# Last weight split of each residual product moved between the scalings of the layer norm, and the mean matmul of the down products four blocks later

## The chip, the cores and the metric

The kernel runs on one core of a Trainium2 chip. The metric is the device time of one execution in microseconds (us). The engines named below are TensorE (PE in the rows, with PEld for its weight loads), VectorE (DVE), ScalarE (ACT), GpSimd (POOL) and the queue of SyncE (SP), which issues the weight transfers.

## What is computed

Two transformer-like blocks run one after the other on 256 tokens of width 1024, all in float32. The first block has two layers, each with a mixer and a feed-forward part, and a layer norm behind each of the four:

```python
for i in range(DEPTH):
    mix = s5_mixer(h, ...) if i % N_MIXERS == 0 else stick_breaking_mixer(h, ...)
    h = layer_norm(DEEPNORM_ALPHA * h + mix, ln_mix_g[i], ln_mix_b[i])
    h = layer_norm(DEEPNORM_ALPHA * h + swiglu_ffn(h, ffn_w_gu[i], ffn_w_down[i]),
                   ln_ffn_g[i], ln_ffn_b[i])
```

The second block has two hybrid layers (window attention beside an mLSTM, then a squared-ReLU feed-forward) with RMS norms. The change touches the four layer norms of the first block alone. They are numbered n = 0 (behind the product with `ssm_w_out`), 1 (behind the first down product), 2 (behind `sb_w_o`) and 3 (behind the second down product).

## The kernel before

**Chunks.** Each weight matrix is cut into chunks of 128x2048 numbers, and one long series of chunks runs through the whole kernel. The raw ring has three slots (`RING = 3`). SyncE loads a chunk into `raw` (`load_chunk`, L362). ScalarE rounds it to `w_hi` (`split_hi`, L395) once the product that used the slot is done. VectorE computes `w_lo = raw - w_hi` (`split_lo`, L400). TensorE needs both: each product is made of three matmuls, high by high, high by low and low by high (L419 to L421), or of two where the moving operand holds both parts (L429, L430). A load waits until the `w_lo` of the chunk that had the slot before is made. So chunk c's product releases the split of chunk c + 3.

**The residual products.** `ssm_out` and `sb_out` have 4 chunks, `down0` and `down1` 11. Each chunk is worked off in 16 blocks of 128 columns (`resid_blocks`). Eight tiles `res` (128x256) come out. `resid_lo(dve, g, idx)` makes the `w_lo` of chunk idx + 3, counted from the product's first: for the last chunk this is the third chunk of the product that follows the layer norm. VectorE's order is written out by hand in `resid_vector` (L1241).

**The layer norm.** It begins before its product ends. With four tiles done VectorE adds them (`shift_sum`, L1048 and L1050). TensorE turns this sum into a provisional mean (`shift_mean`, L786, one float32 matmul over `prod`), and VectorE subtracts that from all tiles (`shifted_tiles`, L1056 and L1058) before the last four tiles arrive. Once the eighth tile is there, TensorE sums differences and squares (`layer_norm_tensor`, L808 to L818), and ScalarE takes them up: L886 squares the mean difference into `rstd`, L887 copies it to `dm_sb`. VectorE forms the variance (L1124), ScalarE the reciprocal root (L891, L894). Then `layer_norm_vector` runs over four pairs of tiles, each op 128x512:

- `centre(q)`, L1129: `xn` minus `dm_sb`; VectorE waits for its own result behind it
- `scale(q)`, L1134: `xn` times `rstd`. ScalarE's `normed_pair` then writes `res` (L919) and, for the first two pairs, `x_hi` (L928)
- `high(q)`, L1142 and `low(q)`, L1150: `x_hi` of the last two pairs, and `x_lo` of all. For n = 3 these are two ops a pair (L1140, L1119)
- `split(0)`, `split(1)`: the `w_lo` of the chunks four and five of the next product. Their `w_hi` comes from `early_columns` (L936 to L940), which stands behind all four `normed_pair` on ScalarE
- `normalised(0)`, `normalised(1)`, L1162 and L1168: what is left of the two early products

**TensorE meanwhile.** While the norm is computed it multiplies the two first chunks of the next product by tiles that are not yet normalised (`early_tensor`, on `raw_hi` and `raw_lo`). Then comes the third chunk, block by block as `x_lo` arrives; its `w_lo` is the one of the split that the change moves. After it comes the fourth, which needs `split(0)`. Behind the fourth chunk n = 1 has the first scores of the attention (L1324), which need `normalised` of both early products; n = 3 has the gate products (L2363), some chunks later.

Of the kernel before, what the change touches and what calls it, by code (L numbers as in the profile page):

```python
# [246 lines left out]
def stack(nc, w, out):  # L247
# [4 lines left out]
    with ctx:  # L252
# [144 lines left out]
        def split_lo(dve, c, idx, k):  # L397
            s = (c + k) % RING
            dve.wait_ge(hi_done, idx + (c + 1))
            nc.vector.tensor_tensor(w_lo[s][:, :], raw[s][:, :], w_hi[s][:, :].bitcast(F32), ALU.subtract).then_inc(lo_done, 1)  # L400
# [291 lines left out]
        def resid_lo(dve, g, idx):  # L692
            if g.c0 + idx + RING < n_chunks:
                split_lo(dve, g.c0 + RING, idx, idx % RING)
# [88 lines left out]
        def shift_mean(pe, n):  # L783

            pe.wait_ge(s_done, n + 1)
            nc.tensor.matmul(PS[:, 3, 0:T], C("mean_c"), prod[:, 0:T], start=True, stop=True).then_inc(shift_ready, 1)  # L786
# [37 lines left out]
        def resid_tensor(pe, g, n, first=True):  # L824

            if g.shape == "kt8":
                if g.half:
                    for kts in ((0, 4), (4, 6), (6, KT)):
                        for idx in range(2):
                            resid_first(pe, g, kts, idx)  # L830
                elif first:
                    resid_first(pe, g)
                if not g.half:
                    resid_blocks(pe, g, 1)
                if n < 4:
                    resid_blocks(pe, g, 2, 0, 6)
                    shift_mean(pe, n)
                    resid_blocks(pe, g, 2, 6, 16)
                else:
                    resid_blocks(pe, g, 2)  # L840
                resid_blocks(pe, g, 3)
            else:
                for idx in range(g.n):
                    if n < 4 and idx == 6:
                        shift_mean(pe, n)
                    resid_blocks(pe, g, idx)
            if n < 4:
                first = 4 if n in (0, 2) else 5
                early_tensor(pe, n, 0, (0, first))
                layer_norm_tensor(pe, n)  # L850
                early_tensor(pe, n, 0, (first, KT))
                early_tensor(pe, n, 1)
# [269 lines left out]
        def layer_norm_vector(dve, g, n):  # L1122
            dve.wait_ge(rstd_done, 3 * n + 2)
            nc.vector.tensor_tensor(rstd[:, :], PS[:, 3, T:2 * T], rstd[:, :], ALU.subtract).then_inc(v_done, 1)  # L1124
            twice = [t[:, :].unsqueeze(1).to_broadcast([P, 2, T]) for t in (dm_sb, rstd)]

            def centre(q):
                pair = xn[:, 2 * q:2 * q + 2, :]
                nc.vector.tensor_tensor(pair, pair, twice[0], ALU.subtract).then_inc(dve_step, 1)  # L1129
                dve.wait_ge(dve_step, v_count.one())  # L1130

            def scale(q):
                pair = xn[:, 2 * q:2 * q + 2, :]
                nc.vector.tensor_tensor(pair, pair, twice[1], ALU.mult).then_inc(scaled, 1)  # L1134

            def high(q):
                dve.wait_ge(res_normed, KT * n + 2 * q + 2)
                if n == 3:
                    for t in (2 * q, 2 * q + 1):
                        nc.vector.tensor_scalar(x_hi[:, t, :], res[:, t, :], gain(4, t), None, ALU.mult).then_inc(xh_done, 1)  # L1140
                    return
                nc.vector.tensor_copy(x_hi[:, 2 * q:2 * q + 2, :], res[:, 2 * q:2 * q + 2, :]).then_inc(xh_done, 2)  # L1142

            def low(q):
                if n == 3:
                    gained_lo(dve, 4, 2 * q)
                    gained_lo(dve, 4, 2 * q + 1)
                    return
                dve.wait_ge(xh_done, KT * x_index(n) + 2 * q + 2)
                nc.vector.tensor_tensor(x_lo[:, 2 * q:2 * q + 2, :], res[:, 2 * q:2 * q + 2, :],  # L1150
                                        x_hi[:, 2 * q:2 * q + 2, :].bitcast(F32), ALU.subtract).then_inc(xl_done, 2)

            def split(slot):
                e, idx = early_chunks(n)[slot]
                split_lo(dve, e.c0 + RING, idx, idx)

            def normalised(slot):

                e, idx = early_chunks(n)[slot]
                dve.wait_ge(cols_copied, 2 * n + slot + 1)  # L1160
                for m in range(2):
                    ins = nc.vector.scalar_tensor_tensor(out=early[:, slot, m * T:(m + 1) * T], in0=dm_sb[:, :],  # L1162
                                                         scalar=col_sums[:, 2 * slot + m, 0:1],
                                                         in1=early_banks(slot)[:, m, 0:T], op0=ALU.mult, op1=ALU.add)
                ins.then_inc(dve_step, 1)
                dve.wait_ge(dve_step, v_count.one())
                both = early[:, slot, :].rearrange("p (a t) -> p a t", a=2)
                nc.vector.tensor_tensor(both, both, twice[1], ALU.mult).then_inc(early_done, 1)  # L1168

            centre(0)  # L1170
            dve.wait_ge(rstd_done, 3 * n + 3)
            scale(0)
            for q in range(1, 3):
                centre(q)
                scale(q)
            low(0)
            centre(3)
            scale(3)
            low(1)
            high(2)  # L1180
            low(2)
            high(3)
            low(3)
            split(0)
            split(1)
            if n == 3:
                square_sums(dve, 4, 0, 4)
            normalised(0)
            normalised(1)
            if n in (0, 2):  # L1190
                early_gated(dve, n, 0)
                early_gated(dve, n, 1)
# [48 lines left out]
        def resid_vector(dve, g, n):  # L1241
            last = g.n - 1
            held = 2 if g.shape == "kt8" else last
            if g.half:
                half_vector(dve, g, n)
                return
            raw_columns(dve, n)
            if n == 3:
                gate_weights(dve)
            for idx in range(g.n):  # L1250
                for t in range(KT):
                    if g.ends[t][0] != idx:
                        continue
                    if n < 4 and t == 4:
                        shifted_tiles(dve, g, n)
                    if n < 4 and t >= 4:
                        shifted_tile(dve, g, n, t)
                    else:
                        add_tile(dve, g, t)
                    if n < 4 and t == 3:  # L1260
                        dve.wait_ge(resid_done, g.resid0 + 4)
                        shift_sum(dve, n)
                        raw_columns_lo(dve, g, n)
                    if n < 4 and t == 5:
                        pair_shift(dve, n)
                    if n in (1, 3) and t == 7:
                        fold_mean(dve, n, 7)
                    if n < 4 and t >= 4:
                        raw_tile_lo(dve, n, 2 * t - 8)
                        raw_tile_lo(dve, n, 2 * t - 7)  # L1270
                    if n == 6:
                        gained_lo(dve, n, t)
                        if t == 5:
                            square_sums(dve, n, 0, 2)
                        if t == 7:
                            square_sums(dve, n, 2, 4)
                    if n < 4 and t == 5:
                        add_squares(dve, n, 0)
                    if n < 4 and t == 6:
                        square_sums(dve, n, 1, 3)  # L1280
                        fold_mean(dve, n, 6)
                    if n in (0, 2) and t == 7:
                        fold_square(dve, n, 6)
                    if n in (1, 3) and t == 7:
                        fold_square(dve, n, 6)
                        fold_square(dve, n, 7)
                if n >= 4 or idx < held:
                    resid_lo(dve, g, idx)
            if n < 4:
                for idx in range(held, g.n):  # L1290
                    resid_lo(dve, g, idx)
            if n < 4:
                layer_norm_vector(dve, g, n)


# [1846 lines left out]
```

## Time and profile before

| | |
|---|---|
| median of 3 runs | 1345.09 us (1344.32 to 1345.76) |
| the profiled execution | 1345.14 us |
| its span in the profile | 1343.3 us |
| TensorE matmuls busy | 1314.0 us (98%) |
| VectorE busy | 944.0 us (70%) |
| ScalarE busy | 676.2 us (50%) |
| GpSimd busy | 56.7 us (4%) |
| share of the chain that ended last: TensorE, VectorE, ScalarE | 86%, 7%, 4% |
| data moved | 227.81 MB, 170 GB/s |

Times in the rows are us from the start of the span. TensorE is busy nearly throughout, so the question for any edit is where TensorE waits, and what ends last before it goes on. A row of the timeline with "x2" holds two instructions back to back. The time given is that of both, and an instruction may start a little before the one ahead of it has ended. The text calls the time from one start to the next a step.

### The profile page before, as it was taken

To read this page: it belongs to the slowest core of one execution; us is meant where nothing else is said; L and a number is where in the kernel's file an instruction comes from. 1 tells how busy PE (TensorE), PEld (TensorE's weight loads), DVE (VectorE), ACT (ScalarE), POOL (GpSimd) and SP (SyncE) were. 2 spreads that over 40 slices of the span, in tenths; PEclk is the share of its full clock that TensorE was granted. 3 is DMA by queue.
4 is the path that set the end of the run, shared out by engine and by line. 5 is a ranking of instruction groups with operands and counts; after the bars stand their busy time and mean duration, and the time that the engine had idled before them with its cause. 6 is when DMAs were issued, how large, how long until landed. Compare 5 with 4: busy or idle time off the path is not lost.

```text
span 1343.3 us, 25869 instructions
## 1 busy us (share of the span) xinstructions
PE 1314.0 (98%) x10699; PEld 1245.2 (93%) x10699; DVE 944.0 (70%) x1340; ACT 676.2 (50%) x838; POOL 56.7 (4%) x31
## 2 busy tenths in 40 slices
PE   5899999999999999999999999999999999999999
PEld 4599999988999999998989999998898999999988
DVE  8966976657865986657897788775457867877542
ACT  5774643334765653344666545444445554544332
POOL 6910000000000000000000000000000000000000
PEclk9999999999999999999999999999999999999999
DMA  8676486675443576666444456567664535556662
GB/s 157 158 185 185 133 221 184 188 190 180 145 148 96 157 208 185 187 188 176 153 137 147 155 159 217 189 184 192 188 188 127 157 123 192 189 188 187 188 188 63
DMA packets 342809, 227.81 MB, mean 170 GB/s; under 512 B 22616, under 2 KB 337792, under 8 KB 342592
## 3 DMA queue, kind: packets, MB, share of 16 engines
q1 hardware_dynamic: 341200, 226.33, 58.5%
q8 instruction: 67, 1.10, 0.3%
q10 hardware_dynamic: 1520, 0.20, 0.1%
q14 instruction: 22, 0.18, 0.0%
HBM read 224.40 MB, written 1.05 MB: 168 GB/s over the span
## 4 chain that ended last, share of the span: by engine, by line
PE 86%; DVE 7%; ACT 4%; issue 1%; POOL 1%; SPq 0%; DMA 0%; DVEq 0%; ACTq 0%; POOLq 0%
PE PS L419 20%; PE PS L420 20%; PE PS L421 20%; PE PS L429 12%; PE PS L430 6%; DVE w_lo L400 2%; ACT w_hi L395 1%; PE PS L1340 1%; DVE xn L1134 1%; DVE xn L1129 1%; DMA c_rows<-in_ssm_c_re_dram 0%; PE PS L1742 0%; PE PS L2430 0%; PE PS L1324 0%; DVE raw_lo L1089 0%
## 5 line engine op out<-in xcount | busy, mean ns | idle before, releaser
L400 DVE TENSOR_TENSOR w_lo<-raw,w_hi 128x2048 fp32r<-128x2048 f32 x207 | 473.6, 2291 | 144.1 <-ACT w_hi L395 143.3
L419 PE MATMUL PS<-x_hi,w_hi 128*128 128x256 f32 x1792 | 504.1, 281 | 1.0 <-DVE w_lo L400 0.5
L420 PE MATMUL PS<-x_lo,w_hi 128*128 128x256 f32 x1792 | 503.7, 281 | 0.0
L421 PE MATMUL PS<-x_hi,w_lo 128*128 128x256 f32 x1792 | 503.3, 281 | 0.0
L395 ACT ACTIVATE w_hi<-raw 128x2048 fp32r<-128x2048 f32 x207 | 396.4, 1915 | 203.2 <-PE PS L430 139.1
L419 PEld LDWEIGHTS PS<-x_hi,w_hi 128*128 128x128 f32 x1792 | 338.3, 189 | 6.0 <-issue 2.9
L420 PEld LDWEIGHTS PS<-x_lo,w_hi 128*128 128x128 f32 x1792 | 336.6, 188 | 0.1
L421 PEld LDWEIGHTS PS<-x_hi,w_lo 128*128 128x128 f32 x1792 | 336.6, 188 | 0.0
L429 PE MATMUL PS<-hid_both,w_hi 128*128 128x512 f32 x756 | 264.8, 394 | 0.0
L430 PE MATMUL PS<-hid_both,w_lo 128*128 128x256 f32 x756 | 211.8, 280 | 0.0
L429 PEld LDWEIGHTS PS<-hid_both,w_hi 128*128 128x128 f32 x756 | 142.1, 188 | 31.4
L430 PEld LDWEIGHTS PS<-hid_both,w_lo 128*128 128x128 f32 x756 | 142.4, 188 | 0.1
L420 PE MATMUL PS<-hid_both,w_hi 128*128 128x256 f32 x492 | 138.3, 281 | 0.0
L421 PE MATMUL PS<-hid_both,w_lo 128*128 128x256 f32 x492 | 138.2, 281 | 0.0
L419 PE MATMUL PS<-hid_both,w_hi 128*128 128x256 f32 x492 | 137.8, 280 | 0.0
L419 PEld LDWEIGHTS PS<-hid_both,w_hi 128*128 128x128 f32 x492 | 92.9, 189 | 0.9 <-issue 0.7
L420 PEld LDWEIGHTS PS<-hid_both,w_hi 128*128 128x128 f32 x492 | 92.4, 188 | 0.1
L421 PEld LDWEIGHTS PS<-hid_both,w_lo 128*128 128x128 f32 x492 | 92.4, 188 | 0.0
L616 ACT ACTIVATE gate_sb<-PS 128x256 f32<-128x256 f32 x48 | 18.4, 383 | 139.5 <-PE PS L421 138.2
L619 ACT ACTIVATE gate_sb<-gate_sb 128x512 f32<-128x512 f32 x32 | 20.2, 632 | 96.0 <-DVE gate_sb L672 96.0
L659 DVE TENSOR_TENSOR prod<-PS,gate_sb 128x256 f32<-128x256 f32 x48 | 20.3, 424 | 58.6 <-ACT gate_sb L616 58.6
L704 DVE SCALAR_TENSOR_TENSOR res<-res,PS 128x256 f32<-128x256 f32 x48 | 19.7, 419 | 35.5 <-PE PS L430 20.0
(395 smaller groups left out, 1482.1 us busy)
## 6 DMA issues: line engine op xcount, KB each, us to landing
raw<-in_w_ff_dram SPq DMA_DIRECT2D x128, 512.0 KB, 4.5
raw<-in_ffn_w_gu_dram SPq DMA_DIRECT2D x88, 512.0 KB, 5.1
raw<-in_w_in_dram SPq DMA_DIRECT2D x68, 512.0 KB, 4.6
raw<-in_sb_w_qkv_dram SPq DMA_DIRECT2D x24, 512.0 KB, 4.5
raw<-in_ffn_w_down_dram SPq DMA_DIRECT2D x20, 512.0 KB, 4.5
raw<-in_ssm_w_glu_dram SPq DMA_DIRECT2D x16, 512.0 KB, 5.6
raw<-in_w_out_dram SPq DMA_DIRECT2D x16, 512.0 KB, 4.6
raw<-in_ssm_w_out_dram SPq DMA_DIRECT2D x8, 512.0 KB, 4.5
```

Source lines behind the costliest of these rows:

```text
L395: nc.scalar.activation(w_hi[s][:, :], raw[s][:, :], ACT.Copy).then_inc(hi_done, 1)
L400: nc.vector.tensor_tensor(w_lo[s][:, :], raw[s][:, :], w_hi[s][:, :].bitcast(F32), ALU.subtract).then_inc(lo_done, 1)
L419: nc.tensor.matmul(dst, lhs_hi, r_hi, start=start, stop=False, skip_group_check=True)
L420: nc.tensor.matmul(dst, lhs_hi, r_lo, start=False, stop=False, skip_group_check=True)
L421: return nc.tensor.matmul(dst, lhs_lo, r_hi, start=False, stop=stop, skip_group_check=True)
L429: nc.tensor.matmul(PS[:, bank, :], lhs_hi, both.rearrange("p i t -> p (i t)"), start=start, stop=False, skip_group_check=True)
L430: return nc.tensor.matmul(PS[:, bank, 0:T], lhs_lo, both[:, 0, :], start=False, stop=stop, skip_group_check=True)
L616: nc.scalar.activation(gate_sb[:, k, 0:T], PS[:, bank, T:2 * T], g.func).then_inc(sig_done, 1)
L619: nc.scalar.activation(gate_sb[:, k, :], gate_sb[:, k, :], ACT.Square).then_inc(u_done, 1)
L659: nc.vector.tensor_tensor(prod[:, 0:T], PS[:, bank, 0:T], gate_sb[:, k, 0:T], ALU.mult).then_inc(z_done, 1)
L704: ins = nc.vector.scalar_tensor_tensor(out=res[:, t, :], in0=res[:, t, :], scalar=g.alpha, in1=PS[:, tile_bank(g, t), 0:T], op0=ALU.mult, ...
L1129: nc.vector.tensor_tensor(pair, pair, twice[0], ALU.subtract).then_inc(dve_step, 1)
```

## The change

For all four layer norms, the `w_lo` of the last chunk of the residual product (`resid_lo` of index g.n - 1) is no longer made before `layer_norm_vector`, but inside it, behind the scalings of pairs 0 and 1. The order inside becomes centre 0, centre 1, scale 0, scale 1, the split, centre 2, scale 2, low 0, low 1, centre 3, scale 3, high 2 and so on. For the down products (n = 1 and 3), `shift_mean` moves from ahead of chunk 6 to behind its first four blocks.

```diff
@@ resid_tensor
                 for idx in range(g.n):
                     if n < 4 and idx == 6:
+                        resid_blocks(pe, g, idx, 0, 4)
                         shift_mean(pe, n)
-                    resid_blocks(pe, g, idx)
+                        resid_blocks(pe, g, idx, 4, 16)
+                    else:
+                        resid_blocks(pe, g, idx)
@@ layer_norm_vector
             centre(0)
+            centre(1)
             dve.wait_ge(rstd_done, 3 * n + 3)
             scale(0)
-            for q in range(1, 3):
-                centre(q)
-                scale(q)
+            scale(1)
+            resid_lo(dve, g, g.n - 1)
+            centre(2)
+            scale(2)
             low(0)
+            low(1)
             centre(3)
             scale(3)
-            low(1)
             high(2)
             low(2)
             high(3)
@@ resid_vector
             if n < 4:
-                for idx in range(held, g.n):
+                for idx in range(held, last):
                     resid_lo(dve, g, idx)
-            if n < 4:
                 layer_norm_vector(dve, g, n)
```

## Rows read from the trace of the kernel before

**Rows 1.** The page, busy time of each engine and its share of the span.
```profile
PE 1314.0 (98%) x10699; PEld 1245.2 (93%) x10699; DVE 944.0 (70%) x1340; ACT 676.2 (50%) x838; POOL 56.7 (4%) x31
```

**Rows 2.** Waits of TensorE: line, whom it waited for, total us, times, longest.
```profile
PE PS L786 <- DVE prod L1050: 1.5, 2, 0.7
...
PE PS L2363 <- ACT rstd L894: 0.4, 1, 0.4
```

**Rows 3.** Timeline of TensorE, n = 1: start, duration, line, op, [idle before].
```profile
303.83 0.28 PE L430 MATMUL PS<-hid_both,w_lo 128*128 128x256 f32 x1
...
304.18 0.28 PE L430 MATMUL PS<-hid_both,w_lo 128*128 128x256 f32 x1
305.19 0.70 PE L786 MATMUL PS<-prod,const 128*128 128x256 f32 x2 [0.73 <-DVE prod L1050]
```

**Rows 4.** Timeline of TensorE, the same mean matmul for n = 0.
```profile
133.46 0.28 PE L421 MATMUL PS<-hid_both,w_lo 128*128 128x256 f32 x1
133.58 0.59 PE L786 MATMUL PS<-prod,const 128*128 128x256 f32 x2
```

**Rows 5.** Timeline of VectorE, n = 1, behind the provisional mean.
```profile
308.66 1.28 DVE L1056 TENSOR_TENSOR xn<-res,PS 128x512 f32<-128x512 f32 x2
```

**Rows 6.** Timeline of VectorE, n = 0, through the layer norm.
```profile
146.39 4.49 DVE L400 TENSOR_TENSOR w_lo<-raw,w_hi 128x2048 fp32r<-128x2048 f32 x2
150.80 0.42 DVE L1124 TENSOR_TENSOR rstd<-PS,rstd 128x256 f32<-128x256 f32 x1
...
152.32 0.69 DVE L1134 TENSOR_TENSOR xn<-xn,rstd 128x512 f32<-128x512 f32 x1 [0.50 <-ACT rstd L894]
152.93 0.69 DVE L1129 TENSOR_TENSOR xn<-xn,dm_sb 128x512 f32<-128x512 f32 x1
153.65 0.69 DVE L1134 TENSOR_TENSOR xn<-xn,rstd 128x512 f32<-128x512 f32 x1
...
156.91 0.69 DVE L1134 TENSOR_TENSOR xn<-xn,rstd 128x512 f32<-128x512 f32 x1
```

**Rows 7.** Timeline of ScalarE, n = 0.
```profile
148.31 0.38 ACT L887 ACTIVATE dm_sb<-PS 128x256 f32<-128x256 f32 x1
151.26 0.51 ACT L891 ACTIVATE rstd<-rstd,const 128x256 f32<-128x256 f32 x1 [2.57 <-DVE rstd L1124]
...
158.74 1.92 ACT L395 ACTIVATE w_hi<-raw 128x2048 fp32r<-128x2048 f32 x1
```

**Rows 8.** Timeline of TensorE, n = 0, first matmul of the fourth chunk.
```profile
163.03 0.39 PE L419 MATMUL PS<-x_hi,w_hi 128*128 128x256 f32 x1 [0.26 <-DVE w_lo L400]
```

**Rows 9.** Timeline of VectorE, n = 1, through the layer norm.
```profile
339.21 0.42 DVE L1124 TENSOR_TENSOR rstd<-PS,rstd 128x256 f32<-128x256 f32 x1
...
345.31 0.69 DVE L1134 TENSOR_TENSOR xn<-xn,rstd 128x512 f32<-128x512 f32 x1
...
349.09 4.49 DVE L400 TENSOR_TENSOR w_lo<-raw,w_hi 128x2048 fp32r<-128x2048 f32 x2 [0.22 <-ACT w_hi L395]
```

**Rows 10.** Timeline of ScalarE, n = 1.
```profile
338.58 0.38 ACT L887 ACTIVATE dm_sb<-PS 128x256 f32<-128x256 f32 x1
...
356.64 0.91 ACT L953 ACTIVATE qkv<-early,col_sums 128x256 f32<-128x256 f32 x2 [0.60 <-DVE early L1168]
```

**Rows 11.** Timeline of TensorE, n = 1, first scores.
```profile
357.60 0.70 PE L1324 MATMUL PS<-qkv 64*128 64x256 f32 x4
```

**Rows 12.** Timeline of VectorE, n = 3, the last scale and the next splits.
```profile
654.67 0.69 DVE L1134 TENSOR_TENSOR xn<-xn,rstd 128x512 f32<-128x512 f32 x1
...
658.70 4.49 DVE L400 TENSOR_TENSOR w_lo<-raw,w_hi 128x2048 fp32r<-128x2048 f32 x2
```

**Rows 13.** Timeline of TensorE, n = 3, first matmul of the fourth chunk.
```profile
661.04 0.39 PE L419 MATMUL PS<-x_hi,w_hi 128*128 128x256 f32 x1
```

**Rows 14.** The page, DMA issues: name, queue, count, KB each, us to landing.
```profile
raw<-in_ffn_w_gu_dram SPq DMA_DIRECT2D x88, 512.0 KB, 5.1
```

**Rows 15.** Busy time by stretch: us, busy of each engine, TensorE's clock, DMA share, GB/s.
```profile
54.00:66.00 12.00, 8.61 (x120) 5.91 (x119) 11.72 (x68) 11.31 (x15) 10.31 (x4) 1.00 0.58 138
```

## The prediction

> **What bounds the kernel now.** I read the busy shares first. TensorE is busy 98% of the span, VectorE 70%, ScalarE 50% [rows 1], so VectorE's work costs only where TensorE has run out of work in front of it. Then come TensorE's waits. Around the layer norms few are left: 1.5 us in two pieces before the provisional mean of the down products, on VectorE's sum, and 0.4 us before the gate products of n = 3, on a reciprocal root that closes VectorE's chain [rows 2]. The timelines around each norm give the rest. In n = 0, TensorE gets to the fourth chunk and waits for its low half: the matmul starts at 163.03 with idle time before it [rows 8], and n = 2 repeats this. In n = 3 the fourth chunk starts at 661.04 [rows 13], 0.05 behind the end of its `w_lo` (658.70 + 2.29, half of the pair's 4.49 and a little [rows 12]). In n = 1 the first scores at 357.60 start 0.05 behind the end of ScalarE's last early eviction (356.64 + 0.91) [rows 10, 11]. So in all four norms the chain that TensorE ends up waiting for is one and the same: VectorE's centrings and scalings, ScalarE's `normed_pair` 3, ScalarE's next `w_hi`, VectorE's next `w_lo`. What moves the last scaling, `scale(3)`, moves TensorE.
>
> **Part 1, the mean matmul.** Now TensorE starts the last matmul ahead of it at 304.18 and the mean at 305.19, a step of 1.01 with 0.73 marked idle [rows 3]. Unstalled, in n = 0, that step is 133.58 - 133.46 = 0.12 [rows 4]. The wait is 1.01 - 0.12 = 0.89. One block takes 304.18 - 303.83 = 0.35 [rows 3], so four blocks are 1.40 of work put into a wait of 0.89. It goes wholly, with 0.5 to spare, and the two other steps around the float32 matmul stay, once. What is late next: the mean comes out 1.40 - 0.89 = 0.5 later. VectorE takes it up at 308.66 at the earliest [rows 5], because the split of chunk 5 is queued before; the mean is done at about 305.19 + 0.70, and 0.5 more leaves over 2 us. So nobody is late. Gain 0.89 in n = 1 and the same in n = 3, whose wait is the other half of the 1.5 [rows 2]: **-1.8**.
>
> **Part 2, the split.** A split holds VectorE for a step of (150.80 - 146.39) / 2 = 2.20 [rows 6]. It leaves the place before L1124 and comes back between `scale(1)` and `centre(2)`. I follow the start of `scale(3)`.
>
> n = 0 (n = 2 is the same). (a) L1124 starts at 150.80, as soon as the second split is through. Its input from ScalarE ends at 148.31 + 0.38 = 148.69 [rows 7], and 0.1 passes until VectorE can start. It could start at 148.79, since the first split ends at about 148.6 [rows 6]: -2.01. (b) VectorE idles 0.50 before `scale(0)`; an op that waits for its own predecessor leaves 153.65 - 152.93 - 0.69 = 0.03 anyway, so `centre(1)` fills 0.47 [rows 6]. It covers the root: that is ready 152.32 - 150.80 = 1.52 behind L1124's start, and `scale(0)` now comes 0.33 + 2 x 0.72 = 1.77 behind it (0.72 = 153.65 - 152.93; 0.33 = 152.32 - 0.47 - 0.72 - 150.80) [rows 6]. -0.47. (c) The split: +2.20. (d) `low(1)` goes ahead of `centre(3)`; an op of 128x512 behind which nothing waits has a step of 152.93 - 152.32 = 0.61 [rows 6]: +0.61. Sum: -2.01 - 0.47 + 2.20 + 0.61 = **+0.33**. `scale(3)` goes from 156.91 to 157.24; `w_hi` starts 158.74 - 156.91 = 1.83 behind it [rows 6, 7], as nothing else holds ScalarE, and TensorE's 163.03 becomes 163.36. What goes on the way are short waits for `x_lo` inside the third chunk. They don't count, as TensorE only waits longer at the fourth. Two norms: **+0.7**.
>
> n = 1. The step that pays in n = 0 is missing. L1124 starts at 339.21 [rows 9] behind one split, but its input ends at 338.58 + 0.38 = 338.96 [rows 10] and can be used at 339.06. The split lies beside ScalarE's and TensorE's work now; without it VectorE stands idle there. (a) is -0.15, (b) -0.47, (c) +2.20, (d) +0.61: **+2.19**. `scale(3)` goes from 345.31 to 347.50, the splits from 349.09 to 351.28 [rows 9], the last eviction and the scores by as much, 357.60 to 359.79 [rows 10, 11]. TensorE gets to the fourth chunk about when its `w_lo` is there now (349.09 + 2.29 = 351.38), so it already loses this time there.
>
> n = 3. The same, but `low` is two smaller ops. (d) I take as 0.8, between the 0.61 of one op and twice the 0.42 of L1124's size [rows 6]. `scale(3)` then goes 2.4 later. The next `w_lo` starts 658.70 - 654.67 = 4.03 behind it now [rows 12]; in n = 0 and 1 ScalarE's `w_hi` allows 1.83 + 1.92 + 0.03 = 3.78 [rows 6, 7, 9], so 0.25 is VectorE's own queue and is given back: **+2.15**, less nothing, since TensorE stands at this `w_lo` already [rows 13]. The gate products' root follows from the same chain, so their wait neither grows nor absorbs.
>
> Other users of the moved split. Its own product, the third chunk, starts in n = 0 no earlier than its `x_lo`, and the split is done about 2 us before; in n = 1 it ends at 344.3 and the chunk starts at about 345.8. Its end also frees a slot for a load on SyncE's queue: 3.2 later in n = 0, 5.1 in n = 1. The load lands in 5.1 [rows 14], and ScalarE reads it only in the third split behind the norm, behind those that start at 158.74 [rows 7]. The loads queued after it each wait for a later split anyway. I take 0, at most 0.5 a norm.
>
> **The sum.** 0.33 + 2.19 + 0.33 + 2.15 - 1.78 = +3.2. The profiled execution took 1345.14 for a span of 1343.3, which becomes 1346.5, so 1348.4. The median of the runs, 1345.09, is 0.05 below: 1348.3. The terms that no row shows are VectorE's pick-up time (0.03 to 0.15 for each norm) and the step of `low` for n = 3 (0.61 to 0.84): together 1347.8 to 1348.9.
>
> **The rivals.** *A, the cover holds in part.* In n = 1 and 3 the third chunk's waits for `x_lo` and the later chain overlap more kindly than I add, or in n = 0 and 2 the split costs nothing because the fourth chunk's idle (0.26 marked [rows 8]) goes: 0.3 each there, 0.25 each in n = 1 and 3. For it: in n = 0 the sum is a difference of larger numbers. Against: every step is from a row. 3.2 - 1.1 = +2.1: 1347.2. *B, faster.* In n = 1 and 3 TensorE has work in front for the whole 2.2, and the wait stays hidden. Then part 1 alone is left: 1345.1 - 1.8 + 0.7 = 1344.0, and 1343.3 if n = 0 and 2 are free too. It decides from a cover of 1.3 us a norm. For it: TensorE has two early chunks and the third in front. Against: it starts the fourth in n = 3 right at the end of `w_lo` [rows 12, 13], and in n = 1 no wait could be that short by chance at the scores [rows 10, 11]. The cover is 0. *C, part 1 gives nothing:* the sum is later too, or TensorE runs into the next wait: 1350.1. Against: VectorE's tile 3 hangs on a block that lies before. *D, the clock.* In the stretch in which TensorE is busy 8.61 of 12.00 us its granted clock stays 1.00, the higher level of 2.4 GHz [rows 15]; the new waits are 2.2 us in pieces. If it fell, the third chunk (48 matmuls, about 5.7) at half speed would add 5.7 in n = 1 and 3: 1360. The Trainium skill, "TensorE: Matmul & The Clock Gate", Part 1 on the clock gate, says that the clock drops to its lower level once TensorE has been idle; by that rule longer waits would be paid twice. The stretch above doesn't show a drop after idle time of this size, and the sum is made without it.
>
> **How the numbers follow.** Forecast 66% (1347.8 to 1348.9, 1348.3), A 20%, B 5%, C 8%, D 1%. About 0.2%, 2.7 us, is what a measurement of this kernel can tell from no change, so slower begins at 1347.8. Slower: 66% less 3 at the edge, plus C and D, 72%. Same: A and the edge, 23%. Faster: B, 5%. The range leaves out B, D and the top of C: 1346.6 to 1349.6.
>
> **What would show it.** TensorE's wait at L786 gone in n = 1 and 3, with the mean's first user unmoved. L1124 2.0 earlier in n = 0 and 2 behind L887, 0.15 earlier in n = 1 and 3, with VectorE idle for over 2 us before it. The wait at the fourth chunk 0.3 longer in n = 0 and 2. In n = 1 and 3 a new wait of about 2 us before the fourth chunk, on `w_lo`. Wrong would be: the fourth chunk of n = 1 starting less than 1 us later against L887 than now, a split under 2 us, or a clock below 1.00.

## The result and the profile after

The changed kernel takes 1348.0 us (median of 14 runs, 1346.84 to 1349.81), the kernel before beside it 1345.34 us (14 runs, 1344.32 to 1345.94). The ratio is 1.0019, with a 95% interval of 1.0012 to 1.0026: slower by 2.7 us, where +3.2 was forecast. Its own profiled execution took 1346.84 us for a span of 1345.0.

The page has the same busy times to within 1.4 us, against [rows 1]. The work is the same, and what changed is who waits:

```profile
span 1345.0 us, 25869 instructions
PE 1314.3 (98%) x10699; PEld 1246.6 (93%) x10699; DVE 944.5 (70%) x1340; ACT 676.7 (50%) x838; POOL 56.8 (4%) x31
```

TensorE's waits (line, whom it waited for, total us, times, longest). The wait of L786 [rows 2] is gone. In its place stand four waits for `w_lo`, one before the fourth chunk of each norm:

```profile
PE PS L419 <- DVE w_lo L400: 4.5, 4, 1.3
...
PE PS L2367 <- ACT rstd L897: 0.4, 1, 0.4
```

The kernel before had two such waits, in n = 0 and 2:

```profile
PE PS L419 <- DVE w_lo L400: 0.5, 2, 0.3
```

Lines behind L840 are three or four higher than before: L1127 is the old L1124, L1132 and L1137 are `centre` and `scale`, L1153 is `low`.

TensorE at the mean matmul of n = 1. The step to L786 is 0.12 now, where it was 1.01 [rows 3], and the one behind it 0.24:

```profile
304.64 0.28 PE L430 MATMUL PS<-hid_both,w_lo 128*128 128x256 f32 x1
304.76 0.59 PE L786 MATMUL PS<-prod,const 128*128 128x256 f32 x2
305.00 0.58 PE L429 MATMUL PS<-hid_both,w_hi 128*128 128x512 f32 x1
```

VectorE in n = 0, which answers to [rows 6]. The second split no longer stands before L1127. It comes behind the two scalings, and VectorE waits for nobody up to `centre(3)`:

```profile
145.18 2.29 DVE L400 TENSOR_TENSOR w_lo<-raw,w_hi 128x2048 fp32r<-128x2048 f32 x1
147.51 0.43 DVE L1127 TENSOR_TENSOR rstd<-PS,rstd 128x256 f32<-128x256 f32 x1
147.85 1.41 DVE L1132 TENSOR_TENSOR xn<-xn,dm_sb 128x512 f32<-128x512 f32 x2
149.29 1.29 DVE L1137 TENSOR_TENSOR xn<-xn,rstd 128x512 f32<-128x512 f32 x2
150.50 2.29 DVE L400 TENSOR_TENSOR w_lo<-raw,w_hi 128x2048 fp32r<-128x2048 f32 x1
...
154.03 1.29 DVE L1153 TENSOR_TENSOR x_lo<-res,x_hi 128x512 fp32r<-128x512 f32 x2
155.24 0.69 DVE L1132 TENSOR_TENSOR xn<-xn,dm_sb 128x512 f32<-128x512 f32 x1
155.96 0.69 DVE L1137 TENSOR_TENSOR xn<-xn,rstd 128x512 f32<-128x512 f32 x1
```

VectorE in n = 1, against [rows 9]. The place that the split left is now idle time, 2.78 us:

```profile
337.14 0.42 DVE L1127 TENSOR_TENSOR rstd<-PS,rstd 128x256 f32<-128x256 f32 x1 [2.78 <-ACT dm_sb L890]
...
340.14 2.29 DVE L400 TENSOR_TENSOR w_lo<-raw,w_hi 128x2048 fp32r<-128x2048 f32 x1
...
345.60 0.69 DVE L1137 TENSOR_TENSOR xn<-xn,rstd 128x512 f32<-128x512 f32 x1
```

TensorE at the fourth chunk of n = 0, 1 and 3. The marked idle time was 0.26 in n = 0 [rows 8] and none in n = 3 [rows 13]. In n = 1 it was none either, as the row behind these three, from the kernel before, shows:

```profile
162.08 0.38 PE L419 MATMUL PS<-x_hi,w_hi 128*128 128x256 f32 x1 [1.02 <-DVE w_lo L400]
...
351.72 0.39 PE L419 MATMUL PS<-x_hi,w_hi 128*128 128x256 f32 x1 [1.15 <-DVE w_lo L400]
...
662.74 0.39 PE L419 MATMUL PS<-x_hi,w_hi 128*128 128x256 f32 x1 [1.35 <-DVE w_lo L400]
```

```profile
351.66 0.28 PE L419 MATMUL PS<-x_hi,w_hi 128*128 128x256 f32 x1
```

**Where the time went, stage by stage.** Both kernels issue the same 10699 matmuls. So one can take the start of the same matmul in two traces and subtract. The difference at seven places (100, 170, 330, 370, 480, 640 and 690 us of the kernel before) gives what each stage, the stretch between two of them, added. A minus sign is time gained. "n=0" to "n=3" are the stages with the four layer norms, "mean1" and "mean3" those with the mean matmul of the two down products. The first number is the lead or lag with which the first block's products are reached, before anything that was changed. Worked out in this way, in us against the trace of before:

```
kernel        at 100    n=0   mean1    n=1    n=2   mean3    n=3   behind 690
changed        -1.21  +0.25  -0.95  +2.19  +0.27  -0.99  +2.15   +0.00
after_again    -0.24  +0.25  -0.96  +2.21  +0.26  -0.98  +2.15   +0.05
mean_only      +1.18  -0.01  -0.94   0.00   0.00  -0.95  +0.01    0.00
split_only     -0.11  +0.27  +0.15  +2.21  +0.26  +0.14  +2.15   +0.02
keep13         -0.52  +0.25  -0.95  +1.36  +0.27  -0.99  +1.07   +0.03
low_back       -0.12  -0.35  -0.97  +1.59  -0.31  -1.00  +1.59   -0.03
joined         +0.26  -0.35  -0.97  +0.07  -0.34  -0.98  +0.09    0.00
centre_mean    +0.75  +0.07  -0.97  +0.06  +0.06  -0.95  +0.08   +0.03
keep02         +1.17  +1.36  -0.99  +2.20  +1.36  -0.99  +2.13   +0.01
best           -0.37  -0.33  -0.97  +0.01  -0.34  -0.98  +0.02    0.00
```

For the changed kernel the stages add up to 0.25 - 0.95 + 2.19 + 0.27 - 0.99 + 2.15 = +2.92. Less the lead of 1.21 at the start, that is the +1.7 between the two spans. The medians differ by 2.7.

### The profile page after: what moved, and what is told of

Same layout as the page of the kernel before. It is cut to its first block, busy times and chain, and to the rows that moved or that the text cites. A ratio compares the mean times of both kernels' runs of the same rounds, so it can differ in the third digit from the quotient of the medians.

```text
span 1345.0 us, 25869 instructions
## 1 busy us (share of the span) xinstructions
PE 1314.3 (98%) x10699; PEld 1246.6 (93%) x10699; DVE 944.5 (70%) x1340; ACT 676.7 (50%) x838; POOL 56.8 (4%) x31
## 3 DMA queue, kind: packets, MB, share of 16 engines
HBM read 224.40 MB, written 1.05 MB: 168 GB/s over the span
## 4 chain that ended last, share of the span: by engine, by line
PE 89%; DVE 7%; ACT 3%; issue 1%; DMA 0%; SPq 0%; DVEq 0%; ACTq 0%
PE PS L419 21%; PE PS L420 21%; PE PS L421 21%; PE PS L429 13%; PE PS L430 7%; DVE w_lo L400 1%; ACT res L922 1%; PE PS L1344 1%; DVE xn L1132 1%; DVE run L2267 1%; ACT w_hi L395 1%; DVE xn L1137 1%; DVE PS L2215 0%; DVE terms L2262 0%; DVE lag L2200 0%
```

## The experiments

Each was timed beside the kernel before, of which the medians were 1345.26 for the first four, 1345.31 for the next four and 1345.51 for the last. Ratios are to the kernel before, with their 95% interval.

**The mean matmul alone.** The kernel before with the first hunk of the diff.

> Only the mean matmul of the down products moves, the split stays where it was. Theory (the four norms carry the slowdown, the mean matmul gives back): the wait of 0.89 us before L786 goes in n = 1 and 3, and nothing is late for it: 1.8 to 1.9 us faster than the kernel before, and TensorE 0.9 to 1.0 ahead from n = 1 on. Rival C (the wait only moves on): within 0.3 us of before, with a new wait on TensorE or VectorE behind the mean.

Measured: 1343.39, ratio 0.9985 (0.9976 to 0.9994), so 1.9 us faster. Both mean stages give 0.94 to 0.95, and no other stage moves by more than 0.01. Rival C falls.

**The split alone.** The changed kernel without the first hunk.

> Only the split and the two reorderings in the layer norm, the mean matmul stays. Theory: +0.3 in n = 0 and 2, +2.2 in n = 1 and 3, so 4.8 to 5.0 us slower than before. Rival A (cover in part): 3.7 to 4.0. Rival B (hidden in n = 1 and 3): under 1.

Measured: 1350.36, ratio 1.0034 (1.0022 to 1.0046), 5.1 us slower. The four norms are those of the changed kernel. A and B fall. The stages of the two mean matmuls lose 0.15 each, in many small steps and not at L786; the cause is open.

**The split kept in its old place in n = 1 and 3.**

```diff
@@ resid_vector
-                for idx in range(held, last):
+                for idx in range(held, last if n in (0, 2) else g.n):
                     resid_lo(dve, g, idx)
@@ layer_norm_vector
             scale(1)
-            resid_lo(dve, g, g.n - 1)
+            if n in (0, 2):
+                resid_lo(dve, g, g.n - 1)
```

> The changed kernel, but in n = 1 and 3 the split stands again before L1127, where VectorE idles for 2.8 us; n = 0 and 2 and the mean matmul stay as changed. Theory (the idle time there is what made the old place free): each of n = 1 and 3 gives back about 2.05 of its 2.2; against before +0.27 twice, +0.1 twice and -1.9, so 1.1 to 1.3 us faster than before and about 4 faster than the change. Rival (the cost lies in the reordering of centrings and low(1), not in the split): no more than 1.5 us faster than the change, so still slower than before.

Measured: 1346.53, ratio 1.0009 (1.0000 to 1.0018). That is 1.3 slower than before, at the edge of no change, where 1.2 faster was expected. Against the changed kernel it is 1.65 faster, so the rival's number (1.5 at most, still slower than before) is the nearer one. Its reading is borne out too: the run joined, below, only puts `low(1)` back and takes away nearly all of what is left in n = 1 and 3. n = 1 and 3 still cost 1.36 and 1.07 where 0.1 was expected. VectorE's timeline in n = 1 shows why:

```profile
341.70 0.69 DVE L1137 TENSOR_TENSOR xn<-xn,rstd 128x512 f32<-128x512 f32 x1
342.41 0.69 DVE L1153 TENSOR_TENSOR x_lo<-res,x_hi 128x512 fp32r<-128x512 f32 x1
344.12 0.69 DVE L1153 TENSOR_TENSOR x_lo<-res,x_hi 128x512 fp32r<-128x512 f32 x1 [1.02 <-ACT x_hi L931]
344.73 0.69 DVE L1132 TENSOR_TENSOR xn<-xn,dm_sb 128x512 f32<-128x512 f32 x1
```

`low(1)` ahead of `centre(3)` costs its own 0.61 only as long as `x_hi` of pair 1 is there. With the split in front it was. Without it VectorE stands 1.02 us at `low(1)`, and `centre(3)` behind it stands too. So half of what leaving out the split would give is taken by another wait: a new one, in a place where the changed kernel has none.

**The changed kernel once more.**

> The changed kernel once more, beside the others on the same chip. Its profiled execution was 1.2 us ahead before the first norm was reached. Theory (chance in the first 70 us): another execution differs there by up to a microsecond either way, and every norm shows the same steps as before: about +0.3, +2.2, +0.3, +2.15 and twice -0.95. Rival (the change speeds up the start): the start is ahead again by 1.2 us. Time 2.5 to 3.2 us over before.

Measured: 1348.18, ratio 1.0020 (1.0011 to 1.0029), 2.9 us slower. Every stage up to 690 us repeats to within 0.02, and at 100 us the lead is 0.24 and not 1.21. So the start differs by chance, and the change doesn't speed it up. A part of what differs is in TensorE's clock. Here is the first profiled execution of the changed kernel (stretch, busy of each engine, TensorE's clock, DMA share, GB/s), behind a wait of 2.98 us for a transfer:

```profile
61.94 2.95 PE L1818 MATMUL PS<-toep,u_in 128*32 128x128 f32 x49 [2.98 <-DMA toep<-toep]
```

```profile
62.00:64.00 2.00, 2.00 (x40) 2.00 (x44) 1.97 (x14) 1.95 (x3) 1.92 (x2) 0.50 0.37 65
64.00:66.00 2.00, 2.00 (x65) 2.00 (x61) 1.89 (x3) 1.91 (x4) 0.64 (x1) 0.78 0.00 0
344.00:354.00 10.00, 8.59 (x70) 8.11 (x69) 9.03 (x11) 5.82 (x10) 0.00 (x0) 1.00 0.41 133
655.00:665.00 10.00, 8.37 (x67) 7.97 (x68) 9.51 (x16) 8.19 (x15) 0.00 (x0) 1.00 0.37 116
```

The clock stood at 0.50 there, the lower level of 1.2 GHz, and at 1.00 in the norms of n = 1 and 3. In after_again and in the kernel before it stayed at 1.00 between 54 and 76 us. Of the eleven traces of this study it fell between 60 and 73 us in six.

What a fall costs can be read in single traces. In mean_only the 96 matmuls of L1835 take 4.49 us from 68.70 on, with the clock at 0.50 from 70 to 72 us, where the kernel before takes 2.87 for the same work (its L1832) at 1.00. Measured by the same matmul in both traces, mean_only is 0.10 behind ahead of them and 1.18 behind at 100 us. Measured in the same way, the fall costs 1.05 in centre_mean, 0.34 in joined, 0.20 in keep02 and 0.10 in split_only. keep02 had another fall at about 30 us and was 1.4 behind at 40 us. The lead of the changed kernel doesn't come from the clock: it was 1.15 ahead at 59 us, before its clock fell. So the clock is a part of the spread and not the whole of it.

**low(1) behind scale(3) again.**

```diff
             low(0)
-            low(1)
             centre(3)
             scale(3)
+            low(1)
```

> The changed kernel with low(1) behind scale(3) again; split and mean matmul as changed. Theory (everything ahead of scale(3) on VectorE moves the fourth chunk one for one): scale(3) comes 0.61 earlier in n = 0, 1 and 2 and 0.80 in n = 3, where VectorE's own queue keeps 0.35 of it back: 0.6 three times and 0.45, so 2.2 to 2.3 us faster than the change, 0.3 to 0.8 slower than before. Rival (TensorE is held by x_lo, so a later low(1) costs what it gives): within 0.5 of the change.

Measured: 1345.73, ratio 1.0003 (0.9994 to 1.0013), 0.4 slower than before and 2.3 faster than the change. By stage 0.60, 0.60, 0.58 and 0.56 come back. The theory holds for the first three to within 0.03; n = 3 gave 0.56 for 0.45. So `x_lo` of pair 1 does not set the end of these stages. The time itself can't be told from that of the kernel before.

**Both: the split moved in n = 0 and 2 alone, and low(1) back.**

> As keep13 (the split moved in n = 0 and 2 alone), but with low(1) behind scale(3) again. In keep13 VectorE idled 1.02 and 0.92 us before low(1), until ScalarE had written x_hi of pair 1. Theory (low(1) ahead of centre(3) costs 0.6 where the split fills that time, and 1.7 where it doesn't): scale(3) comes 1.7 earlier than in keep13 in n = 1 and 3 and 0.6 in n = 0 and 2; against before -0.3 twice, -0.3, -0.5 and -1.9 for the mean matmul, so 3.0 to 3.5 us faster than before. Rival (the early stage of n = 1 and 3 is bound elsewhere): no more than 2.5 faster than before.

Measured: 1342.46, ratio 0.9979 (0.9970 to 0.9988), 2.85 faster than before: a little less than expected. n = 0 and 2 give 0.35, as expected, but n = 1 and 3 give nothing (+0.07, +0.09) where 0.3 and 0.5 were expected from `centre(1)`. The stages add up to -2.5, which is the rival's figure: n = 1 and 3 are held by something else, and the next run shows by what.

**centre(1) ahead, nothing else inside the norm.** The kernel before with the mean matmul moved and:

```diff
             centre(0)
+            centre(1)
             dve.wait_ge(rstd_done, 3 * n + 3)
             scale(0)
-            for q in range(1, 3):
-                centre(q)
-                scale(q)
+            scale(1)
+            centre(2)
+            scale(2)
```

> The kernel before with the mean matmul moved and centre(1) ahead of the wait for the root; the split stays where it was in all four norms, low(1) too. Theory (step a and c of the prediction cancel to +0.2 in n = 0 and 2, so the split's new place is worth nothing anywhere, and only centre(1) gives something): -0.47 in n = 0, 2 and 3, -0.3 in n = 1, where the early eviction waits no more and TensorE's own work sets the scores, -1.9 for the mean: 3.4 to 3.8 us faster than before. Rival (the split's place gives something in n = 0 and 2): slower than the run joined by 0.5 or more.

Measured: 1343.67, ratio 0.9989 (0.9979 to 0.9998), 1.6 faster than before, and the mean matmul's 1.9 is all of that. The expectation was out by 1.8 at least: `centre(1)` ahead costs 0.06 to 0.08 in each norm. The rival holds, as this kernel is 1.2 slower than joined. VectorE in n = 0 did get ahead. From L1127 to `scale(3)` it takes 5.76 here (151.55 to 157.31), against 6.11 before (150.80 to 156.91 [rows 6]). But ScalarE's `w_hi` doesn't follow:

```profile
151.55 0.42 DVE L1127 TENSOR_TENSOR rstd<-PS,rstd 128x256 f32<-128x256 f32 x1
...
153.33 1.29 DVE L1137 TENSOR_TENSOR xn<-xn,rstd 128x512 f32<-128x512 f32 x2
...
157.31 0.69 DVE L1137 TENSOR_TENSOR xn<-xn,rstd 128x512 f32<-128x512 f32 x1
```

```profile
154.06 1.09 ACT L922 ACTIVATE res<-xn,vec 128x256 f32<-128x256 f32 x2 [1.09 <-DVE xn L1137]
155.24 0.63 ACT L931 ACTIVATE x_hi<-res 128x512 fp32r<-128x512 f32 x1
155.78 1.08 ACT L922 ACTIVATE res<-xn,vec 128x256 f32<-128x256 f32 x2
156.96 0.63 ACT L931 ACTIVATE x_hi<-res 128x512 fp32r<-128x512 f32 x1
157.49 2.06 ACT L922 ACTIVATE res<-xn,vec 128x256 f32<-128x256 f32 x4
...
159.57 1.92 ACT L395 ACTIVATE w_hi<-raw 128x2048 fp32r<-128x2048 f32 x1
```

The second fence is ScalarE. From its first `res` to `w_hi` it runs through without a wait, 159.57 - 154.06 = 5.51. It starts with `scale(0)`, and that comes 153.33 - 151.55 = 1.78 behind L1127, against 1.52 before. So the `w_hi` comes 8.02 behind L1127, against 158.74 - 150.80 = 7.94 before [rows 6, 7]: later by 0.08, and the stage measured +0.07. In the kernel before the same run of ScalarE took 158.74 - 153.05 = 5.69, with no idle time marked in it either. So ScalarE had 0.18 to gain from an earlier `scale(3)`, and a `scale(0)` that is 0.26 later costs it more.

**The split kept in its old place in n = 0 and 2.** The mirror image of keep13.

> The changed kernel, but in n = 0 and 2 the split stands again before L1127; moved in n = 1 and 3 alone. Theory: in n = 0 and 2 L1127 comes 2.0 later, the 2.2 of the split go, and low(1) then waits 1.0 to 1.1 for ScalarE's x_hi: +0.9 each against the change, so 1.6 to 2.0 slower than it and 4.4 to 5.0 slower than before. Rival (the split's time is what counts, the wait for x_hi hides it): within 0.5 of the change.

Measured: 1350.24, ratio 1.0040 (1.0026 to 1.0053), 4.9 slower than before and 2.1 slower than the change. n = 0 and 2 cost 1.36 for 0.25, so 1.1 more for the 0.9 expected. In these norms the split's new place is the better one for this order.

**The sum of the parts that give.** Joined, with n = 1 and 3 in the order of before:

```diff
             centre(0)
-            centre(1)
+            if n in (0, 2):
+                centre(1)
             dve.wait_ge(rstd_done, 3 * n + 3)
             scale(0)
+            if n in (1, 3):
+                centre(1)
             scale(1)
```

> The run joined, but n = 1 and 3 keep the whole order of the kernel before inside the layer norm; n = 0 and 2 have the split behind scale(1), centre(1) ahead and low(1) behind scale(3); the mean matmul is moved. Theory (the steps of the stages add up, and in n = 1 and 3 centre(1) ahead only makes scale(0) later for ScalarE): -0.35 in n = 0 and 2, 0.0 in n = 1 and 3, -0.95 twice for the mean matmul, so 2.6 us faster than before by the stages, 1342.7. Rival (centre(1) ahead gives something in n = 1 and 3 that the stages hide): +0.1 or more over the run joined in each of them.

Measured: 1342.57, ratio 0.9979 (0.9970 to 0.9988), 2.9 faster than before and as fast as joined within the noise. By stage -0.33, +0.01, -0.34 and +0.02, with -0.97 and -0.98 for the means: -2.6, as added up beforehand. The rival falls, as n = 1 and 3 are 0.06 and 0.07 better than in joined. Both runs beat the kernel before and the changed one.

## Why the prediction was right

**Reading the bound: right.** The chain over `scale(3)`, ScalarE's `w_hi` and VectorE's `w_lo` is what TensorE waits for in all four norms. The marked waits at the fourth chunk went from 0.26 to 1.02 in n = 0 and appeared in n = 1 and 3, with 1.15 and 1.35. Where the time shows was foreseen less well. The wait of n = 0 was to grow by 0.3 and grew by 0.76, since the third chunk got through 0.5 sooner. In n = 1 and 3 a wait of about 2 us was forecast; 0.67 and 0.85 of the loss came already inside the third chunk, in waits for `x_lo`. And in n = 1 of the kernel before TensorE was not at the edge there: the `w_lo` ended at 349.09 + 2.29 = 351.38 [rows 9], and the chunk started at 351.66 without idle time. The first scores had no such slack, and they set that stage.

**Part 1: right, slightly too small.** Forecast -0.89 for each, measured -0.94 to -1.00. The missing part, 0.05 to 0.11, is no more than what the matmul itself takes longer behind a wait. In the kernel before, the matmul behind L786 started here:

```profile
305.54 0.58 PE L429 MATMUL PS<-hid_both,w_hi 128*128 128x512 f32 x1
```

So after a wait the step from L786 (305.19 [rows 3]) to the next one was 0.35, and unstalled it is 305.00 - 304.76 = 0.24. The first matmul of the fourth chunk shows the same: in n = 1 its step is 351.95 - 351.72 = 0.23 behind the wait, and 351.78 - 351.66 = 0.12 in the kernel before. A stall costs 0.1 more than its idle time here. Nobody was late, as forecast: the run with this part alone moved no other stage.

**Part 2, n = 0 and 2: right.** Forecast +0.33, measured +0.25 to +0.27. The pick-up of ScalarE's result was the term that no row showed. It took 147.51 - 147.48 = 0.03 in n = 0, for 0.1 assumed (147.48 = 147.10 + 0.38 by ScalarE's timeline), and that is the 0.07 by which the forecast was too high. In n = 1 it took the 0.10 assumed (337.14 - 336.66 - 0.38).

**Part 2, n = 1 and 3: right.** Forecast +2.19 and +2.15, measured +2.19 to +2.21 and +2.13 to +2.15. The idle time of 2.78 before L1127 is what the prediction saw: in these norms the old place was free. Step (d) for n = 3, taken as 0.8, is in the timeline 655.90 - 654.31 = 1.59 for the four ops of `low(0)` and `low(1)`, 0.80 a pair. The next `w_lo` came 660.39 - 656.61 = 3.78 behind `scale(3)`, as forecast.

**What was right only in the sum.** Steps (a) to (d) were added as if each stood alone. They hold together because the split keeps VectorE the slower of two engines: in n = 0 of the changed kernel ScalarE stands idle for 0.59 and 1.44 before its last two pairs, waiting for VectorE. Taken out one by one the steps don't hold. Step (b), -0.47 for `centre(1)` ahead, is +0.06 to +0.08 on its own, since then ScalarE's run from `scale(0)` on ends last. The prediction had read that nothing else holds ScalarE [rows 6, 7], and didn't follow ScalarE from its first pair. Step (d), +0.61 for `low(1)` ahead, grows to 344.73 - 342.41 - 0.61 = 1.71 on VectorE without the split (the rows under keep13), since ScalarE's `x_hi` isn't there; taking it back was worth 1.29 in n = 1 and 0.98 in n = 3. My expectations for keep13 and centre_mean failed by 2.5 and by at least 1.8 us, both from this one mistake.

**The rivals.** A, B and C are excluded by the stages, A most narrowly in size (a sum of +2.1) but plainly by stage, since none of the four norms is 0.25 below its term. D: the clock stays at 1.00 through the third and fourth chunks of n = 1 and 3, around waits of 1.15 and 1.35 us. But my evidence against D was weak. I read from one trace that the clock stays up around a wait of 2.42 us at about 60 us [rows 15]. In six of eleven executions it did fall near there. The rule on the clock gate (the Trainium skill, "TensorE: Matmul & The Clock Gate", Part 1) has the clock fall to its lower level after idle time. The first trace of the changed kernel agrees, with its 0.50 behind a wait of 2.98. But idle time alone doesn't sort these traces: in mean_only the clock fell behind waits of 1.60 us at most, and in the kernel before it stayed at 1.00 around the 2.42. No trace here has a fall in a norm. I should have given D more than 1%.

**The sum.** Forecast +3.2, stages +2.92, medians +2.7 and, in the second measurement, +2.9. Over all the runs the stages and the medians differ by 0.4 at most, which is well within the start's spread: 1.21 ahead to 1.18 behind over ten traces.

## What to carry to other kernels

Taking a piece of work out of a place gives only as much as the next operation can then start earlier. Here the same edit gave 2.0 us in two norms, where the input of the next operation was long there, and 0.15 in the other two, where it came just as the split ended; putting the split back cost 2.2 in all four. Where two engines hand pairs of tiles to each other, a step's price holds only for the order it was read in. Before adding up reorderings, follow both engines to the point where they meet again, since the one that isn't last now is last after a gain of a few tenths. And subtract the starts of the same matmul in two traces: stages repeated to within 0.02 us, while the times of one kernel spread over 1.2 to 3.9 us.

## What the runs showed of the hardware that I had not expected

A matmul that had waited held TensorE 0.11 us longer up to the next one than one that had not: 0.35 for 0.24 us at L786, 0.23 for 0.12 at the fourth chunk. And what differs by chance between the eleven traces is made in their first 80 us: there they part by up to 2.4 us, and behind them no stage differs by more than 0.05 between the two traces of the changed kernel. Executions without a trace spread further, and where they do isn't shown. TensorE's clock, which fell to 0.50 at about 60 to 73 us in six of eleven executions of nearly the same program, is a part of it: 0.1 to 1.1 us in the five traces where its cost can be read. What makes the rest of the spread stays open.
